# Expert weights of a mixture-of-experts block loaded as four transfers with 32 KB and 16 KB rows instead of twelve with 8 KB and 4 KB rows

## What is computed

```python
u = x @ w1[e] + b1[e]                 # w1[e]: 1024 x 2048, 8 MiB
y = clamped_swiglu(u) @ w2[e] + b2[e] # w2[e]: 1024 x 1024, 4 MiB
```

## Time and profile before

| | |
|---|---|
| Median of 3 runs | 1405.98 us (1401.76 to 1407.37) |
| Profiled execution | 1398.37 us; span 1396.6 us, 1.8 us around it |
| PE (TensorE matmul) busy | 1268.7 us, 91% of the span |
| DMA over the span | 449.74 MB, mean 322 GB/s |
| Expert weights | 384 transfers of 1024 KB, median 22.4 us from issue to landing |

### The profile page before, as it was taken

One profiled execution on the slowest core, in us unless ns is written; L12 is line 12 of the kernel. 1 busy time (PEld: TensorE's weight loads), 2 busy tenths in 40 slices (PEclk: granted clock), 3 DMA queues, 4 the chain that ended last, 5 costly groups with the idle time before them and its releaser, 6 DMA issues.

```text
span 1396.6 us, 24155 instructions
## 1 busy us (share of the span) xinstructions
PE 1268.7 (91%) x10310; PEld 654.2 (47%) x10310; DVE 324.6 (23%) x553; ACT 200.0 (14%) x319; POOL 59.5 (4%) x29
## 2 busy tenths in 40 slices
PE   6999999999997999899888989888889988889986
PEld 5887888899944333333222333222333322333322
DVE  1114474145532211211111211111111111121112
ACT  4113131122212100110000110000110000010001
POOL 0000000065201000000000000000000000000000
PEclk9999999999997999999999999999999999999999
DMA  8341443510155999999999999999999999999995
GB/s 299 133 168 61 151 150 121 185 51 10 48 195 222 418 419 416 416 419 418 418 419 416 417 418 418 419 418 417 416 418 418 418 418 418 416 417 419 419 418 226
DMA packets 94751, 449.74 MB, mean 322 GB/s; under 512 B 8081, under 2 KB 9105, under 8 KB 61841
## 3 DMA queue, kind: packets, MB, share of 16 engines
q1 hardware_dynamic: 92656, 445.60, 79.1%
q10 hardware_dynamic: 2048, 3.43, 0.9%
HBM read 447.95 MB, written 1.05 MB: 321 GB/s over the span
## 4 chain that ended last, share of the span: by engine, by line
PE 52%; DMA 25%; SPq 18%; issue 2%; DVE 2%; ACT 1%; DVEq 0%; ACTq 0%
DMA ring<-in_exp_w 25%; SPq L318 17%; PE ps L367 17%; PE ps L624 9%; PE ps L654 8%; PE ps L423 4%; PE ps L591 3%; PE ps L582 2%; PE ps L532 2%; PE ps L432 2%; PE ps L425 2%; PE ps L635 1%; DVE work L1179 1%; PE ps L644 1%; PE ps L374 0%
## 5 line engine op out<-in xcount | busy, mean ns | idle before, releaser
L624 PE MATMUL ps<-ring,work 128*64 128x512 f32 x2048 | 480.5, 601 | 74.2 <-DMA ring<-in_exp_w 74.2
L624 PEld LDWEIGHTS ps<-ring,work 128*64 128x64 f32 x2048 | 131.9, 136 | 405.1 <-DMA ring<-in_exp_w 224.1
L367 PE MATMUL ps<-work,ring 128*128 128x256 f32 (+1 forms) x1072 | 232.5, 379 | 0.6 <-ACT work L674 0.6
L654 PE MATMUL ps<-ring,work 128*64 128x512 f32 x1024 | 225.1, 592 | 0.0
L367 PEld LDWEIGHTS ps<-work,ring 128*128 128x128 f32 (+1 forms) x1072 | 202.2, 189 | 31.4 <-issue 2.0
L1168 DVE TENSOR_SCALAR work<-ps 128x512 f32<-128x512 f32 x32 | 22.1, 691 | 536.1 <-PE ps L624 536.1
L654 PEld LDWEIGHTS ps<-ring,work 128*64 128x64 f32 x1024 | 72.6, 137 | 129.6 <-issue 129.6
L823 ACT ACTIVATE work<-work 128x512 f32<-128x512 f32 x32 | 20.1, 629 | 774.2 <-DVE work L1168 774.2
L1184 DVE COPY work<-ps 128x512 f32<-128x512 f32 x32 | 22.1, 691 | 208.2 <-PE ps L654 208.2
L591 PE MATMUL ps<-work 64*128 64x512 f32 x264 | 65.6, 615 | 0.8 <-DVE work L1184 0.8
L582 PEld LDWEIGHTS ps<-sel,work 128*128 128x128 bf16 x1584 | 49.2, 99 | 26.1 <-issue 24.2
(11 more groups left out here) (220 smaller groups left out, 804.0 us busy)
## 6 DMA issues: line engine op xcount, KB each, us to landing
ring<-in_exp_w SPq DMA_DIRECT2D x384, 1024.0 KB, 22.4
ring<-in_w_in SPq DMA_DIRECT2D x16, 2048.0 KB, 7.7
ring<-in_w_out SPq DMA_DIRECT2D x2, 2048.0 KB, 7.7
ring<-in_w_in SPq DMA_DIRECT2D x1, 1152.0 KB, 8.5
work<-in_x SPq DMA_DIRECT2D x2, 512.0 KB, 3.9
work<-in_x ACTq DMA_DIRECT2D x2, 512.0 KB, 4.8
out<-work SPq DMA_DIRECT2D x2, 512.0 KB, 2.7
work<-in_exp_b ACTq DMA_DIRECT2D x3, 256.0 KB, 4.2
```

Source lines behind the costliest of these rows:

```text
L367: last = mm(ps[b % 4][0:width, 0:T], chunk(n)[:, k, c0:c0 + width], XN[:, k, :], start=k == 0, stop=k == KT - 1)
L624: last = mm(ps[4 + part][64 * half:64 * half + 64, :], xe[:, k * CAP:(k + 1) * CAP], ring[:, SLOT[k], part * D + half * 512:part * D + hal ...
L654: last = mm(ps[7][64 * half:64 * half + 64, :], lhs, ring[:, SLOT[8 + j], i * D + half * 512:i * D + half * 512 + 512], start=False, stop= ...
```

## The change

Expert weights come in four transfers: two of 4 MiB for w1, 512 rows each, partition p taking the four neighbouring rows 4p to 4p + 3 as one run of 32 KB; and two of 2 MiB for w2, 512 rows each, again four neighbouring rows on a partition, one run of 16 KB. There are four semaphores and four waits of SP in place of twelve. A transfer waits until all of its slots (4 or 2) are free, and TensorE waits for the whole transfer before the first product that reads it. Since slot s of a transfer now holds rows 4p + s, `gather` and the transposes of `actb` take every fourth column (`every_fourth`). `SLOT` is reordered, so that each transfer's slots are neighbours; the two `w_out` chunks go to slots 0 to 3 instead of 4, 5 and 0, 1; and `w_used` is raised by 8 at the end of the recurrence, with the earlier 2 and 1 dropped.

```diff
-        expert_in = [sem(f"expert_in{i}") for i in range(12)]
+        expert_in = [sem(f"expert_in{i}") for i in range(4)]
+        LOADS = [n % 3 for n in range(NIN)] + [0, 1]
         def chunk(n):
-            s = 2 * (n % 3)
+            s = 2 * LOADS[n]
...
+        def buffer_before(n):
+            return max(i for i in range(n) if LOADS[i] == LOADS[n])
-        SLOT = [2, 3, 11, 6, 7, 8, 9, 10, 0, 1, 4, 5]
+        SLOT = [8, 9, 10, 11, 4, 5, 6, 7, 0, 1, 2, 3]
...
-                    sp.wait_ge(blk_done, blocks_until(n - 3))
+                    sp.wait_ge(blk_done, blocks_until(buffer_before(n)))
...
-                for j in range(12):
-                    sp.wait_ge(w_used, it * 12 + j + 1)
-                    if j < 8:
-                        src = exp_w1[0, bass.ds(e, 1), j * P:(j + 1) * P, :].rearrange("a p n -> p (a n)")
-                        dst = ring[:, SLOT[j], :]
-                    else:
-                        src = exp_w2[0, bass.ds(e, 1), (j - 8) * 2 * P:(j - 7) * 2 * P, :].rearrange(
-                            "a (s p) n -> p (a s) n", p=P)
-                        dst = ring[:, SLOT[j], :].rearrange("p (s n) -> p s n", s=2)
+                for j in range(2):
+                    sp.wait_ge(w_used, it * 12 + 4 * j + 4)
+                    src = exp_w1[0, bass.ds(e, 1), j * 4 * P:(j + 1) * 4 * P, :].rearrange(
+                        "a (p s) n -> p (a s n)", s=4)
+                    dst = ring[:, SLOT[4 * j]:SLOT[4 * j] + 4, :].rearrange("p s n -> p (s n)")
                     sp.dma_start(dst, src).then_inc(expert_in[j], 16)
+                for j in range(2):
+                    sp.wait_ge(w_used, it * 12 + 2 * j + 10)
+                    src = exp_w2[0, bass.ds(e, 1), j * 4 * P:(j + 1) * 4 * P, :].rearrange(
+                        "a (p s) n -> p (a s n)", s=4)
+                    dst = ring[:, SLOT[8 + 2 * j]:SLOT[8 + 2 * j] + 2, :].rearrange("p s n -> p (s n)")
+                    sp.dma_start(dst, src).then_inc(expert_in[2 + j], 16)
...
-            pe.wait_ge(blk_done, len(blocks) + 3 * KT)
-            pe.sem_inc(w_used, 2)
...
-                    pe.sem_inc(w_used, 1)
...
-            pe.sem_inc(w_used, 5)
+            pe.sem_inc(w_used, 8)
...
+            def every_fourth(k):
+                return slice(4 * P * (k // 4) + k % 4, 4 * P * (k // 4 + 1), 4)
...
-                            last = mm(ps[6][:, k * CAP:(k + 1) * CAP], H3[:, t, s, k * P:(k + 1) * P],
+                            last = mm(ps[6][:, k * CAP:(k + 1) * CAP], H3[:, t, s, every_fourth(k)],
...
-                        pe.wait_ge(expert_in[k], (it + 1) * 16)
+                        if k % 4 == 0:
+                            pe.wait_ge(expert_in[k // 4], (it + 1) * 16)
...
-                        last = nc.tensor.transpose(ps[4][:, c * P:(c + 1) * P], actb[:, c * P:(c + 1) * P], C("ident"))
+                        last = nc.tensor.transpose(ps[4][:, c * P:(c + 1) * P], actb[:, every_fourth(c)], C("ident"))
...
-                        pe.wait_ge(expert_in[8 + j], (it + 1) * 16)
+                        if j % 2 == 0:
+                            pe.wait_ge(expert_in[2 + j // 2], (it + 1) * 16)
```

More of the change, by code:

```diff
@@ L211, in build @@
         stream += [(w_out, 0, CHUNK), (w_out, CHUNK, CHUNK)]
+        LOADS = [n % 3 for n in range(NIN)] + [0, 1]
         def chunk(n):
-            s = 2 * (n % 3)
+            s = 2 * LOADS[n]
             return ring[:, s:s + 2, :].rearrange("p s c -> p (s c)").rearrange("p (k c) -> p k c", k=KT)
         def chunk_in(n):
-            return slot_in[2 * (n % 3)], 16 * (n // 3 + 1)
+            return slot_in[2 * LOADS[n]], 16 * LOADS[0:n + 1].count(LOADS[n])
+        def buffer_before(n):
+            return max(i for i in range(n) if LOADS[i] == LOADS[n])
         blocks = [(0, 0, P), (0, P, P), (0, 2 * P, 32)]
```

## The result

The changed kernel takes 1383.74 us (median of 4 runs, 1381.59 to 1386.13) against 1403.87 us (4 runs) of the kernel before: ratio 0.9856, 95% interval 0.9825 to 0.9887. Measured again on one chip with more runs, in the first experiment, it is 1383.62 us against 1401.64 us (11 runs), ratio 0.9882 (0.9865 to 0.9900). Against the profiled execution alone the forecast was closer: 1383.4 us expected, 1381.59 us measured.

The account below looks back on a forecast made before the run. The expert loop was taken to be bound by the DMA stream of weights. Terms -25.7 + 5.2 + 5.2 + 0.3 = -15.0 us took the median of 1406.0 us to 1391 us, range 1384 to 1409 us.

Parts of the forecast that it names:

- Base: Whole kernel: the 15.0 us gain was taken from the runs' median, 1406.0 us, with profiled execution and median shifted alike.
- The cost of a row: Expert loop's weight stream: each row costs an engine 8.7 ns; 96 fewer an expert shorten the stream by 25.7 us.
- rival (b): Weight stream: long rows are cut into 8 KB ones or gain nothing, 1408 us; cut at 16 KB, 1395 us; 14%.
- Later start: Loop's start: the first transfer waits for four pieces of expert 0 instead of one, so the stream starts 5.2 us later.
- Later end: Last expert: its last four w1 pieces land together, a loss of 5.2 us in the sum.
- In the loop: Expert loop: SP's waits for four slots cost nothing; PE waits 2.9 us for the second w1 transfer; period 29.3 us.
- rival (d): PE's clock falls to half after idle stretches of 2.9 us; falls in the last experts show, 1396 to 1401 us; 10%.
- The seven waits of 0.55 us: Expert loop before the change: PE's waits for the next w1 piece, claimed to go with the change.
- Ahead of the loop: Before the loop: nothing is late; x loads sharing engines with 32 KB rows count 0, at worst some 5 us.
- Strided reads: gather's weight loads and the transposes: stepped reads cost 0.3 us, counted once in the last expert; at most 4.1 us an expert.
- Rival (a): Expert loop: strided reads make PE the bound, from 3.0 us more an expert; 1428 us as median at the upper bound; 8%.
- Rival (c): Weight stream: the rows' places in HBM slow it; at 411 GB/s, 25 us slower, 1431 us; 6%.

Follow-up runs that it names:

- the first experiment: The changed kernel run again with no edit, beside the kernel before on the same chip: 1383.62 us against 1401.64 us, ratio 0.9882.

## Why the prediction was wrong, point by point

**Base, 4.3 us of the miss.** This is the step that failed. 1391 = 1406.0 - 15.0, and the time came out at 1383.7, 7.3 us lower. The median of before came down from 1405.98 us in three runs to 1401.64 in eleven, with the changed kernel at 1383.7 and 1383.6 us both times. From 1401.6 us the same sum gives 1386.6 us, inside the range. "The profiled execution was 7.6 us under that median; I shift both alike" was the step: a three-run median that stands 7.6 us from its own profile is an uncertain base, and the range should have carried some 4 us below for it. The terms of the sum, next, were off by 1.2 us in all (-16.2 measured in the loop against -15.0); the 1.8 us that remain no trace explains.

**The cost of a row, 2.4 us.** This is the term of the sum that was mis-sized: 8.7 ns a row, measured 9.4. The two windows gave 8.3, the 2 KB rows 9.5, and I took a value near the first. The period by itself cannot part row from byte; the periods with 128, 80, 64 and 32 rows do. -25.7 us should have been -28.1. The line through three sizes held on to 32 KB, so rival (b), a cut at 8 or 16 KB, is refuted, and a row's price does not depend on its length from 4 to 32 KB.

**Later start:** 5.2 expected, 5.3 measured. **Later end:** 5.2 + 0.3 expected, 6.6 measured as what is left. Part of that was in the forecast's own times: 1381.8 us is 5.7 us later than the old end with the shorter stream and the later start (1396.6 - 25.7 + 5.2 = 1376.1), and the sum put 5.2. From k = 4 of the last expert to the end it is 1379.8 - 1347.06 = 32.7 us against 32.3 in the forecast (5.2 + 26.8 + 0.3). And k = 4 starts 7.2 us before the stream's end, where the forecast had 1357.8 - 1349.8 = 8.0: the last w1 transfer is usable 0.8 us later after its last byte than assumed. That one engine finishes later than the mean of the 16 would do this; it is not shown. With the stream unchanged, old rows in four transfers show both losses alone, 10.6 us.

**In the loop:** PE's waits at k = 4 are mostly 2.6 and 0.9 us in turn (2.9 expected; for the turns see rival (d)), and the engines stay at full share; the new waits of SP cost nothing, as worked out. "The seven waits of 0.55 us" of the prediction are five in the trace; no term of the sum rests on it. Ahead of the loop nothing was late, the x loads included.

**Strided reads:** 0.37 us an expert in the loads, 0.29 us for PE (0.3 taken, 4.1 at most), hidden. Rival (a) needed 3.0 us and is refuted. By the Trainium skill's rule (SBUF — State Buffer, "Door 1") only the fp32 loads should slow down. They do, from 105 to 142 ns; but the bf16 loads pay too, 5 ns each, so here the measurement decides against the rule.

**Rival (c)** is refuted: partitions' rows 32 KB apart run at 430 to 431 GB/s as one long row and, in pieces of 8 KB, at 428 once the stream runs. The slowdown that the Trainium skill gives for a pitch of 512 KiB and more (DMA: Bandwidth & Descriptors, "Latency and other measured facts") does not show at 32 KiB.

**Rival (d)** came, in a smaller form. The trace has 16 waits of 2.6 us at k = 4. After 13 of them the products take 8.5 to 8.8 us in place of 7.09, up to 1.7 us lost, with a granted clock of 0.56 and 0.59 in the windows 1318:1320 and 1320:1322 us; after three (762.74, 967.27 and 1230.20 us) they take 7.09 us. The PE that lost 1.7 us reaches the next wait later, and that one is 0.9 us with no loss behind it. The losses cost the stream nothing, since PE has 29.22 - 26.37 = 2.85 us of slack an expert, but one in the second last expert delays the end once the data comes early enough, as the run with the split end shows.

## What to carry to other kernels

Where a stream of weights has the DMA engines at full share, count the contiguous rows on each engine: each costs a fixed few nanoseconds (9.4 here, for rows of 4 to 32 KB), so lay the contraction index so that neighbouring rows land on one partition, and let the other operand's columns follow with a step. Choose the size of a transfer apart from that: larger ones (4 MiB for 1 MiB here) bring nothing to a stream that is queued deep, and cost at its two ends, where pieces can be kept small. When a change is worth one per cent, read it between two marks in the trace that bracket the stage, and give the base its own uncertainty.

## What was not expected of the hardware

TensorE's clock went to half after most of the single waits of 2.6 us (13 of 16), for stretches that cost up to 1.7 us each, between products that are otherwise dense. The kernel whose waits in the loop were at most 1.27 us (eight transfers) kept a granted clock of 1.00 over the same 600 us; the one with the same rows in four transfers, with waits up to 2.7 us, had 0.98 and the changed kernel 0.97. Which of the long waits are followed by a fall stays open.

```profile
600.00:1200.00 600.00, 535.08 (x3363) 1.00 1.01 426
```
```profile
600.00:1200.00 600.00, 551.45 (x3356) 0.97 1.00 430
```

And a stream can start slower than it goes on: over 8 us near its start it ran at 397 GB/s in the kernel before (444 to 452 us), at 393 in the changed kernel (448 to 456 us) and at 391 in the run with all of expert 1 in pieces (446 to 454 us), the engines at a share of 0.98 to 1.00. It is no rule: with old rows in four transfers the second window of 2 us already shows 426 GB/s. The cause is not shown.
